# A transformer layer with product-key retrieval on one core: the expert table's loads split over two DMA queues, and two kinds of stores moved one block behind the loads

## The reference, cut to what matters

```python
def one(args):
    hb, ib, wb = args
    a = jnp.einsum('td,thkd->thk', hb, u[ib], preferred_element_type=jnp.float32)
    coef = (wb * jax.nn.gelu(a, approximate=False)).astype(v.dtype)
    return jnp.einsum('thk,thkd->td', coef, v[ib])
```

## Time and profile before

| | |
|---|---|
| median of three executions | 5060.66 us |
| the profiled execution, its own time | 5068.84 us |
| its span | 5067.2 us |
| busy TensorE, VectorE, ScalarE, GpSimd | 87%, 60%, 27%, 31% |
| mean granted clock of TensorE | 0.94 |
| DMA, share of 16 engines' span: hardware queue of SyncE, software queue of GpSimd | 46.3%, 15.2% |
| the pass over u, first transpose to last | 2277.5 to 3847.2 us |

### The profile page before, as it was taken

One profiled execution on the slowest core, in us unless ns is written; L12 is line 12 of the kernel. 1 busy time (PEld: TensorE's weight loads), 2 busy tenths in 40 slices (PEclk: granted clock), 3 DMA queues, 4 the chain that ended last, 5 costly groups with the idle time before them and its releaser, 6 DMA issues.

```text
span 5067.2 us, 58390 instructions
## 1 busy us (share of the span) xinstructions
PE 4391.1 (87%) x21067; PEld 3686.3 (73%) x21067; DVE 3052.9 (60%) x3412; ACT 1381.0 (27%) x1489; POOL 1591.9 (31%) x643
## 2 busy tenths in 40 slices
PE   7899999999979976898777996677777799999997
PEld 2687777777768865778777996677776677777776
DVE  1234565455436535457667995566665677787777
ACT  0322332333321121322223442122222233332222
POOL 0002331000003300224444435677774233333330
PEclk9899999999999988899999998999999899999998
DMA  8325663000116552664444779899997889989895
GB/s 280 91 83 169 181 185 116 30 29 19 35 55 193 179 125 73 151 142 108 109 107 100 167 175 257 266 281 279 280 282 260 304 335 335 336 329 341 327 343 179
DMA packets 716548, 967.20 MB, mean 191 GB/s; under 512 B 137467, under 2 KB 535859, under 8 KB 680371
## 3 DMA queue, kind: packets, MB, share of 16 engines
q1 hardware_dynamic: 675395, 680.41, 46.3%
q0 software_dynamic: 40928, 285.23, 15.2%
q10 hardware_dynamic: 144, 0.52, 0.0%
HBM read 896.84 MB, written 69.22 MB: 191 GB/s over the span
## 4 chain that ended last, share of the span: by engine, by line
DMA 22%; DVE 13%; issue 7%; SPq 5%; PE 4%; ACT 1%; POOL 0%; DVEq 0%; ACTq 0%; POOLq 0%
DMA gel<-gelu_scratch 11%; DMA pu<-in_peer_u_dram 11%; DVE acc L1749 3%; DVE oneJ L1700 3%; DVE pT L1607 3%; SPq L554 3%; DVE vDl L1418 3%; PE pp L115 1%; PE pp L116 1%; PE pp L117 1%; ACT act_g L1075 1%; SPq L559 1%; SPq L608 0%; SPq L615 0%; DVE oneI L1701 0%
## 5 line engine op out<-in xcount | busy, mean ns | idle before, releaser
L115 PE MATMUL pp<-h2h,pTuh 128*128 128x384 f32 x2048 | 736.3, 360 | 270.3 <-POOL pTul L721 269.4
L721 POOL TENSOR_TENSOR pTul<-pT,pTuh 128x1024 fp32r<-128x1024 f32 x256 | 695.5, 2718 | 603.0 <-ACT pTuh L1070 601.6
L116 PE MATMUL pp<-h2l,pTuh 128*128 128x384 f32 x2048 | 711.0, 347 | 0.0
L117 PE MATMUL pp<-h2h,pTul 128*128 128x384 f32 x2048 | 711.0, 347 | 0.0
L115 PE MATMUL pp<-vDh,coh 128*128 128x512 f32 x1536 | 614.6, 400 | 97.6 <-DVE col L1418 97.2
L115 PEld LDWEIGHTS pp<-h2h,pTuh 128*128 128x128 f32 x2048 | 404.8, 198 | 312.8 <-POOL pTul L721 286.3
L116 PE MATMUL pp<-vDl,coh 128*128 128x512 f32 x1536 | 608.7, 396 | 0.0
L117 PE MATMUL pp<-vDh,col 128*128 128x512 f32 x1536 | 607.3, 395 | 0.0
L1607 DVE STREAM_TRANSPOSE pT<-pu 128x1024 f32<-128x1024 f32 x256 | 317.2, 1240 | 449.2 <-DMA pu<-in_peer_u_dram 385.7
L1070 ACT ACTIVATE pTuh<-pT 128x1024 fp32r<-128x1024 f32 x256 | 271.5, 1060 | 1146.7 <-DVE pT L1607 1146.4
L697 POOL TENSOR_TENSOR mbuf<-mbuf,silu 128x2048 f32<-128x2048 f32 x64 | 261.1, 4080 | 1003.6 <-DMA mbuf<-in_w_mod_dram 1002.9
(11 more groups left out here) (329 smaller groups left out, 8152.4 us busy)
## 6 DMA issues: line engine op xcount, KB each, us to landing
pu<-in_peer_u_dram SPq DMA_DIRECT2D x512, 256.0 KB, 5.1
vraw<-in_peer_v_dram SPq DMA_DIRECT2D x128, 1024.0 KB, 9.5
mbuf<-in_w_mod_dram SPq DMA_DIRECT2D x64, 1024.0 KB, 5.9
wraw<-in_w_in_dram SPq DMA_DIRECT2D x48, 1024.0 KB, 8.6
wt<-route_scratch SPq DMA_DIRECT2D x128, 384.0 KB, 9.0
gel<-gelu_scratch SPq DMA_DIRECT2D x128, 384.0 KB, 10.4
wm<-in_w_mod_dram SPq DMA_DIRECT2D x16, 2048.0 KB, 8.8
gelu_scratch<-act_g SPq DMA_DIRECT2D x128, 192.0 KB, 1.9
```

Of the source, the lines that this page charges most:

```text
L115: pe.matmul(out, lh, rh, start=first, stop=False)
L116: pe.matmul(out, lh, rl, start=False, stop=False)
L117: return pe.matmul(out, ll, rh, start=False, stop=last)
L721: pool.tensor_tensor(pTul[s][:, c, :], pT[s][:, c, :], pTuh[s][:, c, :].bitcast(fp32), ALU.subtract).then_inc(u_lo, 1)
```

## The change

The loads of `u` are divided: SyncE issues quadrants 0 and 1 of each block, ScalarE issues quadrants 2 and 3 on its own DMA queue. All four add to the same semaphore as before. ScalarE issues its two DMAs of block i + 3 right behind the high part of half 1 of block i + 1, with no wait of their own; `up_block` and `route_part` do this. On SyncE the store of the gelu goes one block behind: load of i + 2, store of i - 1, load of i + 3, store of i. The route stores of a slot are now at three places (two DMAs, one, one) instead of four, each one block later than the first was, and behind the gelu's store instead of ahead of it; the last four come behind the load of block 67 and the store of block 64, where they were behind the load of block 66.

```diff
             def pre_load(i, s):
                 if not isinstance(i, int) or i >= 2:
                     sp.wait_ge(u_turned, 2 * i - 2)
-                for k in range(4):
+                for k in range(2):
                     sp.dma_start(pu[s][32 * k:32 * k + 32, :, :],
                                  u_quarter[k][bass.ds(i, 1)].rearrange("a s b d -> (a s) b d")).then_inc(u_in[s], 16)
...
             pre_load(0, 0)
             pre_load(1, 1)
-            with sp.Fori(0, P0 // 2) as i:
+            pre_load(2, 0)
+            pre_load(3, 1)
+            pre_store(0, 0)
+            with sp.Fori(1, P0 // 2) as i:
                 for s in range(2):
                     pre_load(2 * i + 2 + s, s)
-                    pre_store(2 * i + s, s)
+                    pre_store(2 * i + s - 1, 1 - s)
...
                     pre_load(i + 2, k % 2)
-                    if k >= 4:
-                        route_store(32 * r + 16, 0, k - 4)
-                    elif not first:
-                        route_store(32 * r, 1, k)
-                    pre_store(i, k % 2)
+                    pre_store(i - 1, (k - 1) % 2)
+                    if k >= 5:
+                        for part in ((0, 1), (2,), (3,))[k - 5]:
+                            route_store(32 * r + 16, 0, part)
+                    elif 1 <= k < 4 and not first:
+                        for part in ((0, 1), (2,), (3,))[k - 1]:
+                            route_store(32 * r, 1, part)
...
             pre_load(LATE + 2, 0)
+            pre_store(LATE - 1, 1)
+            pre_load(LATE + 3, 1)
+            pre_store(LATE, 0)
             for k in range(4):
                 route_store(GROUPS, 1, k)
-            pre_store(LATE, 0)
-            pre_load(LATE + 3, 1)
-            pre_store(LATE + 1, 1)
...
             with sp.Fori(LATE // 2 + 3, NK // 2 - 1) as i:
                 for s in range(2):
                     pre_load(2 * i + 2 + s, s)
-                    pre_store(2 * i + s, s)
+                    pre_store(2 * i + s - 1, 1 - s)
+            pre_store(NK - 3, 1)
...
+            def pre_load(i, s):
+                for k in range(2, 4):
+                    act.dma_start(pu[s][32 * k:32 * k + 32, :, :],
+                                  u_quarter[k][bass.ds(i, 1)].rearrange("a s b d -> (a s) b d")).then_inc(u_in[s], 16)
+
...
+            act.wait_ge(sc_done, 2 * PH)
+            pre_load(0, 0)
+            pre_load(1, 1)
...
             pre_hi(0, 0, 1)
+            pre_load(2, 0)
             pre_hi(1, 1, 0)
...
-            def up_block(i, s, exp=None):
+            def up_block(i, s, exp=None, load=True):
                 pre_hi(i + 1, 1 - s, 1)
+                if load:
+                    pre_load(i + 3, 1 - s)
...
                     pre_hi(i + 1, 1 - s, 1)
+                    pre_load(i + 3, 1 - s)
```

More of the change, by code:

```diff
@@ L363, in layer_kernel @@
         block = ctx.enter_context(nc.Block())
+        u_v = a["peer_u"][0].rearrange("(i j) d -> i j d", j=NK)
+        u_quarter = [u_v[:, :, QD * k:QD * k + QD].rearrange("i (b s) d -> i s b d", s=32) for k in range(4)]
         wmod_v = a["w_mod"][0].rearrange("(c p) n -> p c n", p=P)
@@ L542, in _ @@
             sp.dma_start(iota[:, :], a["k_iota"]).then_inc(iota_in, 16)
-            u_v = a["peer_u"][0].rearrange("(i j) d -> i j d", j=NK)
             v_v = a["peer_v"][0].rearrange("(i j) d -> i j d", j=NK)
-            u_quarter = [u_v[:, :, QD * k:QD * k + QD].rearrange("i (b s) d -> i s b d", s=32) for k in range(4)]
             for ss in g_stored:
@@ L1125, in _ @@
                 route_part(r)
-            with act.Fori(LATE // 2, NK // 2 - 1) as i:
+            with act.Fori(LATE // 2, NK // 2 - 2) as i:
                 for s in range(2):
                     up_block(2 * i + s, s)
+            up_block(NK - 4, 0)
+            up_block(NK - 3, 1, load=False)
             pre_hi(NK - 1, 1, 1)
```

## The result

The changed kernel takes 4869.99 us (median of four, 4869.47 to 4870.13), the kernel before 5060.6 us (four executions, 5060.06 to 5067.99): a ratio of 0.962, 95% interval 0.9603 to 0.9637. The time was forecast at 4900, with a range of 4850 to 4965. The profiled execution's span went from 5067.2 to 4867.8 us, 199.4 us less.

A forecast was written before the change was run, and what follows sets the result against it. A once-per-block loop through load, gelu and store was taken to bound blocks 0 to 39 and, with DMA at 0.93, the late ones. Terms 115 + 0 + 5 + 40 + 1 = 161 us gave 4900 us, range 4850 to 4965.

The forecast's parts named there:

- The loop: Load, transpose, high part, gelu, store, load: one load must land before the next is issued, once per block, 11.18 us.
- Blocks 0 to 39: First stretch, 481 us: VectorE becomes the bound, 347 us at best; gain 115 us, ends 85 and 134.
- the unexplained "issue" ones: First-stretch transpose waits of 59.3 us that the profile doesn't show, counted as late loads beside 74.9 us for loads.
- Blocks 40 to 63: Middle stretch, 287 us: VectorE stays full, route stores still come in time; gain 0, ends -5 and +5.
- After block 63: Later route stores delay block 66's low part, block 67's load avoids 4 MB; gain 5 us, ends -8 and +20.
- Blocks 70 to 127: Late stretch, 675 us: DMA share 0.93 limits the gain; 11.1 us a block, 40 us gained, ends 0 and 60.
- The second floor: Late blocks: GpSimd and VectorE, where both are dense, need 5.4 us per half block, 10.8 us a block.
- Two queues: ScalarE's issues cost nothing, the second queue adds no bandwidth; first loads go out 2 us sooner, 1 us gained.
- everything opens: Rival, chance 0.10: both stages reach their floors, 220 us saved, 4841 us.
- DMA full late: Rival, chance 0.22: late stage and its beginning give nothing, only the first stage counts, 115 + 1 us, 4945 us.
- the loop stays: Rival, chance 0.09: another order still ties load to gelu; only issuing shortens, 0.91 us in 40 + 57 blocks, 4972 us.
- the slower one: Rival, chance 0.04: ScalarE stands at its DMA issues, up to 6.43 us each; 5154 us, deciding from about 5.6 us an issue.

The follow-up runs named there:

- The order alone: Changed kernel with all four load DMAs of a block on SyncE's queue, stores still one block behind: 4866.18 us, ratio 0.9624.
- the queues alone: Kernel before with loads divided over SyncE's and ScalarE's queues, SyncE's stores where they were: 4962.04 us, ratio 0.9807.
- cutting it at ScalarE's link: Kernel before, one queue, stores where they were; gelu of i put ahead of the high part of half 0 of i + 2: 4905.93 us, ratio 0.9696.
- two experiments (4866 and 4873 us with one queue): Changed kernel with all four load DMAs on SyncE's queue, 4866.18 us, or all on ScalarE's, 4872.57 us.
- The kernel with half the load bytes: Changed kernel with late loads of u bringing half of the experts (SyncE's half from block 72, ScalarE's from 75): 4862.9 us, ratio 0.962.

## Why the prediction was right, and where it wasn't

**The loop.** Right. The order alone gives the whole gain, the queues alone leave the loop standing at 9.94 us a block, and cutting it at ScalarE's link gives 148 us of the 188.

**Blocks 0 to 39.** Forecast 115 us, measured 114.3. All of the transposes' waits for loads went, the unexplained "issue" ones among them, so it was right to count these as late loads. The part not gained against the 134 at best is mostly the 17.8 us in which VectorE now waits for TensorE.

**Blocks 40 to 63.** Forecast 0, measured 0.8. (In the code only the first of a slot's four route stores comes a block later, not all of them.) But what held this stretch wasn't the two full engines alone: without GpSimd's low parts beside the one-hots it is 24 us shorter.

**After block 63.** Forecast 5 us, measured about 12.6: the store of block 70's gelu came 130.1 us behind the last one-hot before, and 117.5 after. GpSimd's first gather was 27.9 us behind the last one-hot before and 34.0 after, 6 us later, inside the 8.3 forecast. Something else won more than that: load 67, which now goes out ahead of the route stores, or the loop that is gone in blocks 64 to 70 as well. No run tells which.

**Blocks 70 to 127.** Forecast 40 us with an end of 60, measured 67.5 by the same marks. The step that failed is "At a share of 1, the same packets need 11.84 x 0.93 = 11.0 us a block". The share is the sum of the packets' times, and these aren't fixed. From 3100 to 3500 us, the kernel before, the order alone and the changed kernel:

```profile
3100.00:3500.00 400.00, 290.80 (x1472) 276.10 (x1471) 250.31 (x189) 75.10 (x90) 294.02 (x125) 0.90 0.91 273
3100.00:3500.00 400.00, 328.71 (x1763) 305.36 (x1762) 392.59 (x220) 91.71 (x111) 382.56 (x148) 1.00 1.00 308
3100.00:3500.00 400.00, 330.18 (x1781) 306.55 (x1780) 400.00 (x223) 92.43 (x111) 386.83 (x150) 1.00 0.93 310
```

GB/s by share are 300, 308 and 333. With one queue the packets stayed nearly as long, and the order alone has a share of 1.00 as forecast, just without a loss in time: its floor was somewhat below 11.0 us. An estimate, from a block's 276 GB/s x 11.84 us = 3.27 MB at 308 GB/s, is 10.6 us. It is the second queue, to which the prediction gave nothing, that took the share down to 0.93 at the same pace. The kernel with half the load bytes shows that DMA wasn't the bound of the changed kernel. The second floor, 10.8 us from a dense stretch of the two engines, was the true one, to the tenth; and the mean before was nearer 12.0 than 11.84 us a block in the blocks that have a load ahead of them. So two of the prediction's signs failed: it wanted about 635 us of 675 for this stretch, at a share of 0.98 or more; by 67.5 us less it is some 607, at 0.92.

**Two queues.** Nothing from ScalarE's issues and no time from the second queue: right for the changed kernel, by two experiments (4866 and 4873 us with one queue). The rule of the Trainium skill (DMA: Bandwidth & Descriptors, "Issuing engines are not separate DMA queues"), that issuing from more than one engine only saves issue time, holds for it, too, as far as time goes. Where the DMA engines are full the measurement goes against it and decides: dividing the loads took the rate from 306 to 350 GB/s and was worth 71 us, of which shorter issuing is the smaller part by the estimate above.

**Sum.** Forecast 161 us of span, measured 199.4; in medians 161 against 191. The late blocks are 27.5 of the 38.4 us between the two. By the number the result doesn't choose between the forecast of 4900 us, 30 off, and the rival "everything opens" with 4841, 29 off. The first stretch went as forecast and stayed short of that rival's floor, the late blocks went as the rival had it and a little past its 60 us. That the whole landed in the range owes something to the range's width; "DMA full late" falls, "the loop stays" is what the queues alone would have given (4962 against its 4972), and the slower one needed issues of 5.6 us where the longest was 1.77.

## What to carry to other kernels

When a queue's engine sits waiting most of the time and no engine is full, follow one item around: what does the instruction that it waits for wait for itself? A loop that passes through a load once per item costs the full latency of the load each time, and moving one store or one gelu by one place frees it. A DMA share near 1 isn't a floor until fewer bytes make the kernel faster; and two engines whose instructions get longer when they run together should be added, not taken side by side.

## What the runs showed of the hardware that was not expected

**GpSimd and VectorE in turn.** This holds for some of VectorE's instructions. A dot on VectorE took 4.30 us beside GpSimd's subtraction and 2.25 with that moved away. In the routing stretch one one-hot in eight took up to 2.4 us instead of 0.3. VectorE's transposes got no longer beside GpSimd, 1.26 us at most in the changed kernel. Even GpSimd's gather instruction went from about 0.95 to 2.83 us beside a dot. Putting the subtraction on the engine that was busy all of the time made the kernel 78 us faster, and 104 with the routing stretch.

**Loads divided over two hardware queues have shorter packets.** With gathers on the software queue, and the same loads on two hardware queues instead of one, time per MB fell from 1.02% to 0.79% of the stretch, and the total rose from 306 to 350 GB/s. The changed kernel beside the order alone has it too (a share of 0.93 at 310 GB/s instead of 1.00 at 308), but only where DMA bounded did it show in the time. Why the packets get shorter the runs don't tell.
